# Second score pass of units over 512 keys in 64-row tiles of the TensorE array

## The chip, the cores and the metric

The kernel runs on one core of one Trainium2 chip. The metric is the device time of one execution in microseconds (us), the median of several runs; less is better.

## The reference, cut to what matters

One layer of a decoder trunk over 1024 positions of width 1024. The input is normalised and modulated (adaLN), projected to q, k and v of 8 stick-breaking heads and 8 forgetting heads (64 wide each), a gate path and 8 forget logits. The two kinds of attention give `o_sb` and `o_fx`, which are normalised, gated and projected back.

```python
def block(args):                       # stick-breaking, a block of 128 queries
    qb, i = args
    q_pos = i * Q_BLOCK + jnp.arange(Q_BLOCK)
    z = jnp.einsum('bhqd,bhkd->bhqk', qb, k).astype(jnp.float32) * scale
    causal = key_pos[None, :] < q_pos[:, None]
    log_rem = jnp.where(causal, jax.nn.log_sigmoid(-z), 0.0)
    after = lax.cumsum(log_rem, axis=3, reverse=True) - log_rem
    a = jnp.where(causal, jnp.exp(jax.nn.log_sigmoid(z) + after), 0.0)
    return jnp.einsum('bhqk,bhkd->bhqd', a.astype(v.dtype), v)
...
def block(args):                       # forgetting
    qb, cum_q, i = args
    q_pos = i * Q_BLOCK + jnp.arange(Q_BLOCK)
    logits = jnp.einsum('bhqd,bhkd->bhqk', qb, k).astype(jnp.float32) * scale
    logits = logits + cum_q[..., :, None] - cum[..., None, :]
    causal = key_pos[None, :] <= q_pos[:, None]
    p = jax.nn.softmax(jnp.where(causal, logits, -jnp.inf), axis=-1)
    return jnp.einsum('bhqk,bhkd->bhqd', p.astype(v.dtype), v)
```

## The kernel before

**Number format.** TensorE multiplies numbers of a rounded 32-bit format (fp32r, shown as f32 in the rows). To keep precision each operand is split into a rounded high part and a low rest, and a product is made of several passes that add up in one PSUM bank.

**Work.** The 16 heads form 8 pairs of two heads; even pairs are stick-breaking, odd pairs forgetting. A pair has 16 steps, one per unit g: head a of the pair, block qb (0 to 7) of 128 queries. `unit(g)` (L54) gives pair, head and block. A unit sees n = (qb + 1) * 128 keys, in pieces of up to 512 (`pieces`, L58): blocks 0 to 3 have one piece, blocks 4 to 7 have two, the second one of 128, 256, 384 or 512 keys. There are 128 units, 64 of them with two pieces.

**Scores.** The tile `stacks` (L180) holds for a buffer (p % 2) and a head three slots of 1024 columns over 128 partitions. Slot 0 is q, scaled, with its high part in partitions 0 to 63 and its low part in 64 to 127. Slot 1 is the high part of k in both halves of the partitions, slot 2 the low part of k in both. So the first pass of `scores` (L1314), q against slot 1, contracts over 128 rows and gives q_hi k_hi + q_lo k_hi, and the second pass (L1315), q against slot 2, gives q_hi k_lo + q_lo k_lo. The causal mask is added to the last 128 columns of a unit by a third, bf16, matmul (L1318). Each piece takes one of three PSUM banks in turn (`SCORE`, L224) and waits until the reader of the piece three before has freed it; `s_score` counts the finished pieces.

**Who reads them.** In `scores_out` of ScalarE (L757) a stick-breaking piece goes through two sigmoids (L767, L768); VectorE then scans (L1037) and GpSimd multiplies (L608). In `scores_out` of VectorE (L1033) a forgetting piece gets its forget term and row maximum (L1050), ScalarE takes the exponential (L772), VectorE the reciprocal (L1060), and GpSimd scales the row (L614). TensorE then transposes the probabilities (`transpose_probs`, L1342), ScalarE and VectorE copy them out as high and low part (L800, L1097), and TensorE multiplies them with the values (`values`, L1364).

**Order of the work.** Every engine has a program written out by hand as a loop over the units. On TensorE step g holds: half a projection unit of the next pair (`proj`, 12 matmuls of 512 columns at L1290, L1291, L1295), `scores(g + 2)`, on even steps `values` of the two units before, and `transpose_probs(g)`, which waits for GpSimd's `s_prob`. The last pair has output products (L1376) in place of most projections.

**Where q comes from.** `proj_out` of ScalarE (L717) copies the high part of a finished q projection from PSUM into slot 0 of both heads (L736, L737), then VectorE writes the low part (L1016) and so frees the bank. A q projection comes in two halves of 512 positions, `th` 0 and 1.

**Transfers by GpSimd.** From the end of pair 6 on, GpSimd issues 16 DMAs itself (`load_y_parts`, L573 to L579, and `load_wo`, L584 and L585), between its multiplications for the forgetting units.

Of the kernel before, what the change touches and what calls it, by code (L numbers as in the profile page):

```python
# [25 lines left out]
def hybrid_trunk_kernel(nc, x, c, w_ada_t, b_ada_cols, g_norm_cols, w_in, b_f_col, g_grp_cols, w_out, g_final,  # L26
                        identity, out):
    fp32 = mybir.dt.float32
    fp32r = mybir.dt.float32r
    bf16 = mybir.dt.bfloat16  # L30
    ALU = mybir.AluOpType
    ACT = mybir.ActivationFunctionType

    P = 128
    SEQ, D = x.shape
    HD = 64
    DC = D // P
    TB = SEQ // P
    HALF = 512
# [8 lines left out]
    SCALE = HD ** -0.5  # L48
    LOWEST = -3e38

    def is_sb(g):
        return (g // STEPS) % 2 == 0
# [5 lines left out]
    def pieces(g):  # L58

        n = (g % TB + 1) * P  # L60
        return [(a, min(a + HALF, n)) for a in range(0, n, HALF)]
# [49 lines left out]
    for g in all_units + [UNITS]:  # L111
        p, i = g // STEPS, g % STEPS
# [45 lines left out]
    with ctx:  # L158
        def sb(name, shape, dt=fp32):
            return ctx.enter_context(nc.sbuf_tensor(name, shape, dt))  # L160
# [17 lines left out]
        w_lo = sb("w_lo", [P, 2, DC, P], fp32r)  # L178

        stacks = sb("stacks", [P, 2, 2, 3, SEQ], fp32r)  # L180

        v_stack = sb("v_stack", [P, 2, 2, TB, P], fp32r)

# [14 lines left out]
        ident_bf = sb("ident_bf", [P, P], bf16)  # L198
        mask_f = sb("mask_f", [P, 2, P])
        mask_bf = sb("mask_bf", [P, 2, P], bf16)  # L200
# [59 lines left out]
        s_score = sem("s_score")  # L260
# [419 lines left out]
        def _(act):  # L680
# [36 lines left out]
            def proj_out(u, first=True, second=True):  # L717

                p, kind, th = units[u]
                bank = PROJ[proj_bank(u)]  # L720
                st = p % 2
                cols = slice(th * HALF, (th + 1) * HALF)
                if first:
                    act.wait_ge(s_proj, u + 1)
                if kind == "k":
                    for a in range(2):
                        src = bank[a * HD:(a + 1) * HD, :]
                        if a == 0 and first or a == 1 and second:
                            nc.scalar.activation(stacks[0:HD, st, a, 1, cols], src, ACT.Copy)
                            nc.scalar.activation(stacks[HD:P, st, a, 1, cols], src,  # L730
                                                 ACT.Copy).then_inc(s_phi if a else s_phk, 1)
                    return
                if not first:
                    return
                if kind == "q":
                    nc.scalar.activation(stacks[0:HD, st, 0, 0, cols], bank[0:HD, :], ACT.Copy, scale=SCALE)  # L736
                    nc.scalar.activation(stacks[0:HD, st, 1, 0, cols], bank[HD:P, :], ACT.Copy,  # L737
                                         scale=SCALE).then_inc(s_phi, 1)
                elif kind == "v":
                    if p == 0:  # L740
                        act.wait_ge(s_ada, 2 * DC)
                    if p >= 2:
                        act.wait_ge(s_tfree, T_ITEM["SS", p - 2, 0])
                    nc.scalar.activation(VT[:, cols], bank, ACT.Copy).then_inc(s_phi, 1)
                elif kind == "g":
                    if p == LAST:
                        act.wait_ge(s_wlo, len(blocks))
                    elif p >= 1:
                        act.wait_ge(s_yst, 16 * p)
                    else:  # L750
                        act.wait_ge(s_f, 4)
                    nc.scalar.activation(gate_of(p)[:, cols], bank, ACT.Sigmoid).then_inc(s_phi, 1)
                else:

                    nc.scalar.activation(CUM[1][0:8, cols], bank[F_LO:F_LO + 8, :], ACT.Copy).then_inc(s_phi, 1)
# [109 lines left out]
            for g in range(UNITS):  # L865
                p, i = g // STEPS, g % STEPS
# [389 lines left out]
        def _(pe):  # L1256
# [42 lines left out]
            def scores(g):  # L1299
                p, a, qb = unit(g)  # L1300
                q = stacks[:, p % 2, a, 0, qb * P:(qb + 1) * P]
                if g % STEPS == 0:
                    pe.wait_ge(s_plo, LO_UNITS[p, "k", 1])
                for j, (c0, c1) in enumerate(pieces(g)):
                    n = S_PIECE[g, j]
                    bank = SCORE[(n - 1) % 3]
                    if n > 3:
                        before = piece_list[n - 4]
                        if is_sb(before[0]):
                            pe.wait_ge(s_sig, SB_PIECE[before])  # L1310
                        else:
                            pe.wait_ge(s_logit, FX_PIECE[before])
                    diagonal = c1 == (qb + 1) * P
                    nc.tensor.matmul(bank[:, 0:c1 - c0], q, stacks[:, p % 2, a, 1, c0:c1], start=True, stop=False)  # L1314
                    last = nc.tensor.matmul(bank[:, 0:c1 - c0], q, stacks[:, p % 2, a, 2, c0:c1], start=False,  # L1315
                                            stop=not diagonal)
                    if diagonal:
                        last = nc.tensor.matmul(bank[:, c1 - c0 - P:c1 - c0], ident_bf[:],  # L1318
                                                mask_bf[:, 0 if is_sb(g) else 1, :], start=False, stop=True)
                    last.then_inc(s_score, 1)  # L1320

            def next_bank(item):
                n = T_ITEM[item]
# [178 lines left out]
```

## Time and profile before

| | us |
|---|---|
| median of 3 runs | 832.3 (832.14 to 835.11) |
| span of the profiled execution, first to last instruction | 828.7 |
| around that span in the profiled execution, taken from median less span | 3.6 |
| TensorE (PE) busy | 720.7 |
| weight loads (PEld) busy, beside PE | 604.4 |
| VectorE (DVE) busy | 490.9 |
| ScalarE (ACT) busy | 408.4 |
| GpSimd (POOL) busy | 390.7 |

The profiled execution's own time is not listed apart from its span; the last difference stands in for it. PE is TensorE's matmuls, PEld its loads of the stationary operand, DVE VectorE, ACT ScalarE, POOL GpSimd, SP the SyncE queue. A row of a timeline has the start, the duration, the engine, the line of the code, the operation with output and inputs, the shape, and in brackets the idle time of the engine just before with what ended it. Matmuls are pipelined, so one begins before the one ahead has ended: the pace is read from start to start, the duration has the way through the array in it.

### The profile page before, as it was taken

To read this page: it belongs to the slowest core of one execution; us is meant where nothing else is said; L and a number is where in the kernel's file an instruction comes from. 1 tells how busy PE (TensorE), PEld (TensorE's weight loads), DVE (VectorE), ACT (ScalarE), POOL (GpSimd) and SP (SyncE) were. 2 spreads that over 40 slices of the span, in tenths; PEclk is the share of its full clock that TensorE was granted. 3 is DMA by queue.
4 is the path that set the end of the run, shared out by engine and by line. 5 is a ranking of instruction groups with operands and counts; after the bars stand their busy time and mean duration, and the time that the engine had idled before them with its cause. 6 is when DMAs were issued, how large, how long until landed. Compare 5 with 4: busy or idle time off the path is not lost.

```text
span 828.7 us, 10998 instructions
## 1 busy us (share of the span) xinstructions
PE 720.7 (87%) x3936; PEld 604.4 (73%) x3936; DVE 490.9 (59%) x993; ACT 408.4 (49%) x846; POOL 390.7 (47%) x325
## 2 busy tenths in 40 slices
PE   0257965989999999999989989998899899999996
PEld 0146754768887887888777878887788788788884
DVE  1486663776564567756634676565447765545565
ACT  4027333576457555554645555555556465623132
POOL 2244422535866563467476644665556465221100
PEclk9988997999999999999989999999999999999998
DMA  6553332104245431133342411244432308894223
GB/s 185 183 200 148 129 100 40 35 22 86 98 102 138 108 103 26 26 91 102 88 136 57 102 26 26 77 128 127 152 94 67 85 25 304 243 311 166 68 90 128
DMA packets 64390, 91.57 MB, mean 111 GB/s; under 512 B 5448, under 2 KB 39880, under 8 KB 63824
## 3 DMA queue, kind: packets, MB, share of 16 engines
q1 hardware_dynamic: 57216, 72.17, 30.4%
q0 software_dynamic: 5376, 14.68, 5.6%
q10 hardware_dynamic: 1744, 4.02, 1.2%
q8 instruction: 32, 0.52, 0.2%
q14 instruction: 22, 0.18, 0.1%
HBM read 67.23 MB, written 23.63 MB: 110 GB/s over the span
## 4 chain that ended last, share of the span: by engine, by line
PE 34%; DMA 21%; POOL 19%; issue 9%; DVE 9%; ACT 6%; SPq 1%; DVEq 0%; POOLq 0%; ACTq 0%
DMA w_raw<-in_w_in 15%; PE psum L1376 10%; POOL w_lo L540 6%; DMA work<-in_w_ada_t 5%; PE psum L1290 4%; PE psum L1291 4%; PE psum L1295 4%; PE psum L1364 4%; DVE work L1037 3%; PE psum L1342 3%; POOL w_hi L534 3%; POOL work L554 2%; POOL work L608 2%; DVE stacks L1005 2%; POOL work L614 2%
## 5 line engine op out<-in xcount | busy, mean ns | idle before, releaser
L1290 PE MATMUL psum<-h_hi,w_hi 128*128 128x512 f32 x496 | 209.6, 423 | 23.9 <-POOL h_lo L591 13.5
L1295 PE MATMUL psum<-h_hi,w_lo 128*128 128x512 f32 x496 | 197.6, 398 | 0.0
L1291 PE MATMUL psum<-h_lo,w_hi 128*128 128x512 f32 x496 | 197.2, 398 | 0.0
L800 ACT ACTIVATE pt_hi<-psum 128x512 fp32r<-128x512 f32 (+1 forms) x192 | 87.5, 490 | 140.5 <-PE psum L1342 137.3
L1097 DVE TENSOR_TENSOR pt_lo<-psum,pt_hi 128x512 fp32r<-128x512 f32 (+1 forms) x192 | 100.6, 551 | 84.4 <-ACT pt_hi L800 83.4
L608 POOL TENSOR_TENSOR work<-work 128x127 f32<-128x127 f32 (+3 forms) x64 | 77.4, 1211 | 152.2 <-DVE work L1037 152.2
L1290 PEld LDWEIGHTS psum<-h_hi,w_hi 128*128 128x128 f32 x496 | 96.0, 193 | 43.6 <-issue 16.2
L1037 DVE TENSOR_TENSOR_SCAN work<-work 128x128 f32<-128x128 f32 (+3 forms) x64 | 104.1, 1627 | 32.5 <-ACT work L768 32.4
L1342 PE MATMUL psum<-ident,work 128*128 128x128 f32 x576 | 88.8, 282 | 29.9 <-POOL work L614 16.0
L1295 PEld LDWEIGHTS psum<-h_hi,w_lo 128*128 128x128 f32 x496 | 95.5, 192 | 22.2
L1291 PEld LDWEIGHTS psum<-h_lo,w_hi 128*128 128x128 f32 x496 | 96.1, 194 | 16.6
L1342 PEld LDWEIGHTS psum<-ident,work 128*128 128x128 f32 x576 | 63.5, 144 | 32.6 <-POOL work L614 17.3
L540 POOL TENSOR_TENSOR w_lo<-w_raw,w_hi 128x1024 fp32r<-128x1024 f32 x31 | 83.2, 2685 | 2.6
L772 ACT ACTIVATE work<-work,small 128x128 f32<-128x128 f32 (+3 forms) x64 | 49.8, 777 | 64.5 <-DVE small L1055 64.2
L1364 PE MATMUL psum<-pt_hi,v_stack 128*128 128x256 f32 x320 | 81.1, 288 | 0.4
L614 POOL TENSOR_SCALAR work<-work,small 128x128 f32<-128x128 f32 (+3 forms) x64 | 47.9, 749 | 68.6 <-DVE small L1060 68.5
L534 POOL TENSOR_SCALAR w_hi<-w_raw 128x1024 fp32r<-128x1024 f32 x31 | 34.5, 1112 | 94.6 <-DMA w_raw<-in_w_in 92.7
L1364 PE MATMUL psum<-pt_lo,v_stack 128*128 128x256 f32 x320 | 75.6, 283 | 0.0
L781 ACT ACTIVATE spare<-psum 64x256 f32<-64x256 f32 x64 | 24.4, 381 | 93.2 <-PE psum L1364 92.9
L1068 DVE TENSOR_TENSOR work<-psum,spare 64x256 f32<-64x256 f32 x64 | 26.7, 417 | 73.5 <-ACT spare L781 57.7
L1314 PE MATMUL psum<-stacks 128*128 128x512 f32 (+1 forms) x192 | 66.1, 345 | 4.4 <-ACT work L768 2.6
L1315 PE MATMUL psum<-stacks 128*128 128x512 f32 (+1 forms) x192 | 63.8, 345 | 0.0
(141 smaller groups left out, 1291.5 us busy)
## 6 DMA issues: line engine op xcount, KB each, us to landing
w_raw<-in_w_in SPq DMA_DIRECT2D x32, 512.0 KB, 9.4
work<-in_w_ada_t SPq DMA_DIRECT2D x24, 512.0 KB, 9.2
work<-in_x SPq DMA_DIRECT2D x16, 512.0 KB, 6.6
w_split_scratch<-work SPq DMA_DIRECT2D x16, 512.0 KB, 3.4
y_split_scratch<-work SPq DMA_DIRECT2D x10, 512.0 KB, 3.7
work<-forget_scratch SPq DMA_DIRECT2D x8, 512.0 KB, 5.1
work<-in_w_out SPq DMA_DIRECT2D x16, 256.0 KB, 5.6
stacks<-y_split_scratch POOLq DMA_DIRECT2D x4, 1024.0 KB, 6.7
```

Source lines behind the costliest of these rows:

```text
L540: nc.gpsimd.tensor_tensor(lo, w_raw[:], hi.bitcast(fp32), ALU.subtract).then_inc(s_wlo, 1)
L608: nc.gpsimd.tensor_tensor(U[g % 2][:, 0:n - 1], U[g % 2][:, 0:n - 1], R[g % 2][:, 1:n], ALU.mult).then_inc(s_prob, 1)
L800: nc.scalar.activation(pt_hi[:, a:e, (g % 2) * P:(g % 2 + 1) * P], bank, ACT.Copy).then_inc(s_thi, 1)
L1037: nc.vector.tensor_tensor_scan(R[g % 2][:, 0:n][:, ::-1], R[g % 2][:, 0:n][:, ::-1], R[g % 2][:, 0:n][:, ::-1], 1.0, ALU.mult, ALU.bypass) ...
L1097: nc.vector.tensor_tensor(pt_lo[:, a:e, q0:q0 + P], bank, pt_hi[:, a:e, q0:q0 + P].bitcast(fp32), ALU.subtract).then_inc(s_tfree, 1)
L1290: nc.tensor.matmul(bank, hi, h_hi[:, c_, cols], start=(c_ == 0), stop=False)
L1291: last = nc.tensor.matmul(bank, hi, h_lo[:, c_, cols], start=False, stop=(kind == "f" and c_ == DC - 1))
L1295: last = nc.tensor.matmul(bank, lo, h_hi[:, c_, cols], start=False, stop=(c_ == DC - 1))
L1314: nc.tensor.matmul(bank[:, 0:c1 - c0], q, stacks[:, p % 2, a, 1, c0:c1], start=True, stop=False)
L1342: last = nc.tensor.transpose(bank[:, (k - a) * P:(k - a + 1) * P], U[g % 2][:, k * P:(k + 1) * P], ident[:])
L1364: last = nc.tensor.matmul(OUT[:, c0:2 * P], v_stack[:, p % 2, a, k, :], src[:, k, c0:2 * P], start=(k == 0 and n == 0), stop=(k == qb + 1 ...
L1376: last = nc.tensor.matmul(psum[:, bank, :], y_, w_[:, m, cols], start=(j == 0 and k == 0), stop=(j == PAIRS // 2 - 1 and k == 2))
```

## The change

A new tile `q_again` holds the high part of the scaled q once more, in partitions 64 to 127, for both heads and for the positions 512 to 1023 (blocks 4 to 7). ScalarE writes it with two more copies of 64x512 whenever a q projection's half `th` = 1 is copied out.

A unit with two pieces is done in another order and with another second pass. Both pieces' first passes come first, into two banks. Then the second pass of the first piece contracts over partitions 0 to 63 only (q_hi against k_lo), and the second pass of the second piece over partitions 64 to 127 only (q_hi from `q_again` against the upper copy of k_lo). Then the mask. The small term q_lo k_lo is left out for these units. Units with one piece are as before. The number of matmuls is the same: five for a unit with two pieces.

The tile takes 8 KB of every partition (2 x 2 x 512 x 4 bytes). `dynamic_dma_scratch_size=4096` sets aside less of each partition for the descriptors of DMAs that GpSimd issues.

```diff
         stacks = sb("stacks", [P, 2, 2, 3, SEQ], fp32r)
+        q_again = sb("q_again", [P, 2, 2, HALF], fp32r)
...
                 if kind == "q":
                     nc.scalar.activation(stacks[0:HD, st, 0, 0, cols], bank[0:HD, :], ACT.Copy, scale=SCALE)
+                    if th == 1:
+                        for a in range(2):
+                            nc.scalar.activation(q_again[HD:P, st, a, :], bank[a * HD:(a + 1) * HD, :], ACT.Copy,
+                                                 scale=SCALE)
                     nc.scalar.activation(stacks[0:HD, st, 1, 0, cols], bank[HD:P, :], ACT.Copy,
                                          scale=SCALE).then_inc(s_phi, 1)
...
-                for j, (c0, c1) in enumerate(pieces(g)):
+                def whole(j, c0, c1):
                     n = S_PIECE[g, j]
                     bank = SCORE[(n - 1) % 3]
                     if n > 3:
...
-                    diagonal = c1 == (qb + 1) * P
                     nc.tensor.matmul(bank[:, 0:c1 - c0], q, stacks[:, p % 2, a, 1, c0:c1], start=True, stop=False)
-                    last = nc.tensor.matmul(bank[:, 0:c1 - c0], q, stacks[:, p % 2, a, 2, c0:c1], start=False,
-                                            stop=not diagonal)
-                    if diagonal:
-                        last = nc.tensor.matmul(bank[:, c1 - c0 - P:c1 - c0], ident_bf[:],
-                                                mask_bf[:, 0 if is_sb(g) else 1, :], start=False, stop=True)
-                    last.then_inc(s_score, 1)
+                    return bank
+
+                def mask(bank, c0, c1):
+                    return nc.tensor.matmul(bank[:, c1 - c0 - P:c1 - c0], ident_bf[:],
+                                            mask_bf[:, 0 if is_sb(g) else 1, :], start=False, stop=True)
+
+                if len(pieces(g)) == 1:
+                    (c0, c1), = pieces(g)
+                    bank = whole(0, c0, c1)
+                    nc.tensor.matmul(bank[:, 0:c1 - c0], q, stacks[:, p % 2, a, 2, c0:c1], start=False, stop=False)
+                    mask(bank, c0, c1).then_inc(s_score, 1)
+                    return
+                banks = [whole(j, c0, c1) for j, (c0, c1) in enumerate(pieces(g))]
+                first, second = pieces(g)
+                nc.tensor.matmul(banks[0], q[0:HD], stacks[0:HD, p % 2, a, 2, first[0]:first[1]], start=False,
+                                 stop=True).then_inc(s_score, 1)
+                nc.tensor.matmul(banks[1][:, 0:second[1] - second[0]],
+                                 q_again[HD:P, p % 2, a, qb * P - HALF:(qb + 1) * P - HALF],
+                                 stacks[HD:P, p % 2, a, 2, second[0]:second[1]], start=False, stop=False)
+                mask(banks[1], *second).then_inc(s_score, 1)
...
-    nc = bacc.Bacc("TRN2", target_bir_lowering=False, num_devices=1)
+    nc = bacc.Bacc("TRN2", target_bir_lowering=False, num_devices=1, dynamic_dma_scratch_size=4096)
```

How the change moves TensorE's program: unit 6 (pair 0, head 0, block 6, so pieces of 512 and 384 keys), before. L1295 is the end of a projection, L1364 the values of the units before. L1314 and L1315 are the two passes of a piece, L1318 the mask.

```order
L1295 MATMUL psum<-h_hi,w_lo 128x512
L1314 MATMUL psum<-stacks 128x512
L1315 MATMUL psum<-stacks 128x512
L1314 MATMUL psum<-stacks 128x384
L1315 MATMUL psum<-stacks 128x384
L1318 MATMUL psum<-mask_bf,ident_bf 128x128
L1364 MATMUL psum<-pt_hi,v_stack 128x256
```

The same place in the changed program. L1321 is the first pass, L1337 the second pass in the lower rows, L1339 that in the upper rows, L1326 the mask.

```order
L1302 MATMUL psum<-h_hi,w_lo 128x512
L1321 MATMUL psum<-stacks 128x512
L1321 MATMUL psum<-stacks 128x384
L1337 MATMUL psum<-stacks 128x512
L1339 MATMUL psum<-stacks,q_again 128x384
L1326 MATMUL psum<-mask_bf,ident_bf 128x128
L1386 MATMUL psum<-pt_hi,v_stack 128x256
```

The second piece's first pass has moved ahead of the first piece's second pass, and the two second passes stand side by side. Shapes name output partitions and columns, so the 64 rows do not show in them.

ScalarE's program where pair 1's q, half `th` = 1, is copied out, before (L736, L737). L767 and L768 are sigmoids, L781 the copy of values.

```order
L767 ACTIVATE work<-psum 128x256
L768 ACTIVATE work<-psum 128x256
L736 ACTIVATE stacks<-psum 64x512
L737 ACTIVATE stacks<-psum 64x512
L781 ACTIVATE spare<-psum 64x256
```

The same place in the changed program, with the copies at L739, L742 and L744.

```order
L774 ACTIVATE work<-psum 128x256
L775 ACTIVATE work<-psum 128x256
L739 ACTIVATE stacks<-psum 64x512
L742 ACTIVATE q_again<-psum 64x512 x2
L744 ACTIVATE stacks<-psum 64x512
L788 ACTIVATE spare<-psum 64x256
```

Two more copies stand between the two old ones, ahead of the signal that lets VectorE make the low part.

## Rows read from the trace of the kernel before

**Rows 1.** The page: the span in 40 slices, busy tenths (about 21 us each).

```profile
PE   0257965989999999999989989998899899999996
POOL 2244422535866563467476644665556465221100
PEclk9988997999999999999989999999999999999998
```

**Rows 2.** One stretch, 120 to 760 us, busy time of each engine.

```profile
120.00:760.00 640.00, 597.87 (x3375) 504.59 (x3376) 383.44 (x788) 346.30 (x738) 345.40 (x289) 0.98 0.37 103
```

**Rows 3.** Who TensorE waited for, 120 to 760 us: total, times, longest.

```profile
PE psum L1342 <- POOL work L614: 16.0, 9, 5.3
PE psum L1342 <- POOL work L608: 12.4, 4, 8.5
PE psum L1314 <- ACT work L768: 2.6, 2, 1.8
PE psum L1314 <- DVE small L1050: 1.8, 2, 1.6
```

**Rows 4.** Timeline of TensorE, a unit of 512 and 128 keys.

```profile
411.00 0.39 PE L1314 MATMUL psum<-stacks 128*128 128x512 f32 x1
411.23 0.39 PE L1315 MATMUL psum<-stacks 128*128 128x512 f32 x1
411.46 0.22 PE L1314 MATMUL psum<-stacks 128*128 128x128 f32 x1
411.51 0.28 PE L1315 MATMUL psum<-stacks 128*128 128x128 f32 x1
411.63 0.23 PE L1318 MATMUL psum<-mask_bf,ident_bf 128*128 128x128 bf16 x1
```

**Rows 5.** The same, units with second pieces of 256, 384 and 512 keys.

```profile
340.95 0.28 PE L1315 MATMUL psum<-stacks 128*128 128x256 f32 x1
341.07 0.23 PE L1318 MATMUL psum<-mask_bf,ident_bf 128*128 128x128 bf16 x1
...
344.96 0.34 PE L1315 MATMUL psum<-stacks 128*128 128x384 f32 x1
345.14 0.23 PE L1318 MATMUL psum<-mask_bf,ident_bf 128*128 128x128 bf16 x1
...
350.14 0.39 PE L1315 MATMUL psum<-stacks 128*128 128x512 f32 x1
350.37 0.23 PE L1318 MATMUL psum<-mask_bf,ident_bf 128*128 128x128 bf16 x1
```

**Rows 6.** Timeline of weight loads in the unit of rows 4.

```profile
411.23 0.19 PEld L1314 LDWEIGHTS psum<-stacks 128*128 128x128 f32 x1
411.46 0.19 PEld L1315 LDWEIGHTS psum<-stacks 128*128 128x128 f32 x1
```

**Rows 7.** Timeline of TensorE where a projection starts after a wait.

```profile
333.28 0.47 PE L1290 MATMUL psum<-h_hi,w_hi 128*128 128x512 f32 x1 [0.64 <-DVE stacks L1005]
333.58 0.40 PE L1291 MATMUL psum<-h_lo,w_hi 128*128 128x512 f32 x1
```

**Rows 8.** The copy of q by line (L737), and who ScalarE waited for, 120 to 760 us.

```profile
L737 ACT ACTIVATE stacks<-psum x16: 595/596/598, 75.8 to 625.6; 64x512 fp32r<-64x512 f32 x16
...
ACT pt_hi L800 <- PE psum L1342: 129.0, 63, 11.3
```

**Rows 9.** Timeline near 113 us, before the first scores are used.

```profile
111.27 3.38 DVE L954 CUSTOM_DVE_ANT_0 pt_lo<-work 128x1024 fp32r<-128x1024 f32 x1 [3.97 <-DMA work<-in_w_ada_t]
113.62 0.50 PE L1290 MATMUL psum<-h_hi,w_hi 128*128 128x512 f32 x1 [3.97 <-POOL w_lo L540]
```

**Rows 10.** A DMA that GpSimd issues (timeline), and its time to landing (DMA issues).

```profile
730.30 0.80 POOL L584 DMA_DIRECT2D h_lo<-w_split_scratch  x1
...
h_lo<-w_split_scratch POOLq DMA_DIRECT2D x4, 1024.0 KB, 7.7
```

## The prediction

> **What bounds the kernel now.** I read the page's slices first, then the busy time of the stretch in which the units run, then TensorE's waits in it, then its timeline inside single units. The slices show TensorE at 9 tenths or close to it from about 120 us on, at the full clock, while GpSimd moves between 4 and 8 [rows 1]. In the stretch from 120 to 760 us TensorE is busy 597.9 of 640 us, the next engine 383 us [rows 2]. So it stands still for 42.1 us in 640, and 28.4 us of that are 13 waits of the transposes for GpSimd's probabilities [rows 3]. Everything else there is TensorE at its own pace. A nanosecond taken from its stream in this stretch is a nanosecond off the end, unless it is taken just ahead of one of those few waits; a nanosecond added always shows. The change touches only the 64 units with two pieces, which all run in this stretch, 16 of each size.
>
> **Term 1, the second pass of the second piece goes under the first piece's.** The pace is start to start. Before, a pass of 512 keys takes 0.23 us (411.23 to 411.46) and the two passes of a unit's two pieces follow each other [rows 4]. The second pass of the second piece takes 0.12 us for 128 keys (411.51 to 411.63) [rows 4], and 0.12, 0.18 and 0.23 us for 256, 384 and 512 keys (341.07 less 340.95, and so on) [rows 5]. After, it stands in rows 64 to 127 of the array while the first piece's pass of 0.23 us is in rows 0 to 63. If the two run side by side it costs only what it hangs over. The second one cannot start before its weights are in. The nearest row for that lag is the one where a load and the matmul that uses it lie closest: the load of L1315 starts at 411.46 [rows 6] and its matmul at 411.51 [rows 4], 0.05 us. With that lag the passes of 128, 256 and 384 keys end within 0.23 us (0.05 + 0.18 = 0.23), and that of 512 hangs over by 0.05. Saved per unit: 0.12, 0.12, 0.18 and 0.18, together 0.60 us; times 16 is **9.6 us**. Bounds: nothing, if the two do not overlap, and 16 x 0.65 = 10.4 us without any lag.
>
> The Trainium skill, in "TensorE: Matmul & The Clock Gate", section "Measured speedup vs the span model", puts the lag between tiles of different rows at about 4 ns; by it this term would be about 10.3 us. No row of this trace shows matmuls in two row tiles.
>
> **Term 2, changing between 128 and 64 rows.** A changed unit goes from a 128-row first pass to 64-row tiles, and back for the mask: 2 changes x 64 units = 128 changes. The trace before has none, so I bound one. Below: nothing. A change of kind that the trace does have, from an f32 pass to the bf16 mask, costs nothing: 0.12 us after the pass of 128 keys, as the pace of such a pass is elsewhere, and 0.23 us after that of 512 [rows 4, 5]. Above: the array must be empty before it is set up anew. A matmul of 512 keys lasts 0.39 us from start to end and the next starts after 0.23 us [rows 4], so waiting for the end costs 0.16 us; then the weights, which now load under the running matmul [rows 6], come after it, another 0.05 us: 0.21 us. Between them lies the restart after a wait: the first matmul of a projection then takes 0.30 us to the next start, not 0.23 [rows 7], so 0.07 us are lost where weights were not loaded ahead. The three prices times 128 are 0, 9.0 and 26.9 us. I take **0**: the nearest row is the change of format within the same unit, where the next weights load under the running matmul all the same.
>
> **Term 3, the first piece is ready later.** `s_score` for the first piece now comes after the second piece's first pass, 0.05 to 0.23 us later, while the second piece is ready earlier. Its readers are two units ahead of the transposes, so mostly this is slack. It shows only where TensorE ends up waiting for the chain of that unit: 13 waits for GpSimd and a few shorter ones [rows 3]. At most 0.23 us at 15 places, 3.5 us, at least nothing. I take half, **+1.7 us**. The waits for a free score bank are 4.4 us in four places [rows 3], and the new order asks for the second bank only one pass earlier: within this term.
>
> **Term 4, ScalarE's copies.** 16 more copies of 64x512 at 0.596 us [rows 8] are 9.5 us on an engine that is busy 346 of 640 us [rows 2] and waited 129 us for the transposes [rows 8]. In a pair they come as 1.2 us at one step of sixteen, ahead of a bank that the next projection needs two units later. I cost them at nothing; without that cover each pair's step would slip 1.2 us, 8.3 us over seven pairs. The first two copies lie before the stretch, near 102 us, and hold up VectorE's low parts by 1.2 us. VectorE then waits 3.97 us for a load, and TensorE as long for GpSimd's weights, which depend on neither [rows 9]: absorbed.
>
> **Term 5, the smaller scratch.** GpSimd issues 16 DMAs of its own; one takes 0.80 us to issue and lands after 7.7 us [rows 10]. If the space still holds what is in flight, nothing changes, and I take nothing.
>
> **Sum.** 828.7 - 9.6 + 0 + 1.7 = 820.8 us of span, and with the 3.6 us around it **824.4 us**, 7.9 us under the median of 832.3, to which the profiled execution's span is tied by that same 3.6. A measurement of this kernel can tell about 0.5% from no change, 4.2 us.
>
> **Rival 1: the array is emptied at every change of tiling.** The mechanism is that of the upper bound: the 64-row load waits until the 128-row pass has gone through, and the mask's load until both tiles are done. Place: L1321 to L1337 and L1339 to L1326 in each of the 64 units, and nothing covers it, since TensorE is the bound [rows 2]. Price 26.9 us, time 824.4 + 26.9 = **851.3 us**. It breaks even at 7.9/128 = 0.06 us a change and is slower by over 0.5% from 0.095 us on; at 0.12 us it gives 839.8 us. For it: the long way through the array (0.16 us) [rows 4]. Against it: consecutive matmuls with other weights, formats and banks never wait for one another here [rows 4 to 6].
>
> The page "TensorEngine Tiling (Array Packing)" of the Trainium skill, section "Key Properties", says that a change of tiling mode, unlike one of tile, drains the TensorE. It gives no price; no row of this trace shows such a change. By that rule the time is that of this rival, and it is why I do not put it lower than I do.
>
> **Rival 2: only the prefetch of weights is lost at a change.** The array takes the new tiling on the fly, but a load for another tiling does not run under the matmul before. Price 9.0 us by the restart after a wait [rows 7], time **833.4 us**: within 0.5%. It would eat term 1 almost exactly.
>
> **Rival 3: the two 64-row passes run one after the other.** Then the change does not do what it says: as many columns stream as before, term 1 is nothing, and the time is 832.3 + 1.7 = **834.0 us**. For it: every matmul of this trace starts at the earliest when the one ahead has taken its columns. Against it: no two here are in different rows.
>
> **Rival 4: the smaller scratch makes GpSimd wait.** A second issue would wait for the first's landing, 7.7 - 0.8 = 6.9 us, in the four pairs of `load_wo`, ahead of the probabilities that TensorE's transposes need. With some 3 us of slack each this is 16 us: **840 us**. It needs descriptors for some MB in flight at a time, and loads are issued in twos.
>
> **Chances.** The forecast, 43%: it needs two things to go well, and both are what this trace shows of TensorE so far. Rival 1, 30%, anywhere from 0.095 to 0.21 us a change. Rival 2, 20%. Rival 3, 5%. Rival 4, 2%. The likeliest is the forecast, so 824.4. Its own range is 822 (no lag, half of term 3) to 827 (term 3 in full, 1 us of term 4). The whole range must reach into rival 1 to leave out no more than 2 in 10: from 821 to 847, where the top leaves out about the dearest third of it. Faster by over 0.5%: 43%. Within 0.5%: rivals 2 and 3, 25%. Slower by over 0.5%: rivals 1 and 4, 32%.
>
> **What would show it.** In the profile after: L1339 starting about 0.05 us after L1337 in every unit says term 1 is right; 0.23 us says rival 3. The time from L1321 of the second piece to L1337 beyond that pass's own pace (0.05 to 0.12, 0.12, 0.18, 0.23 us), and from L1339 to L1326 beyond what is left of the passes, is term 2: none says forecast, about 0.07 rival 2, 0.1 to 0.21 rival 1. TensorE's waits for GpSimd in 120 to 760 us should grow from 28.4 to about 30 us; if they grow by the whole of term 1, the gain went into the chain of the probabilities. The landing and issue times of L587 and L588 show rival 4. The forecast is wrong if a changed unit, from its first first pass to the matmul after the mask, is not 0.12 to 0.18 us shorter than before.

## The result and the profile after

The changed kernel is slower: 840.9 us median (839.24 to 842.08, 4 runs) against 833.7 us (4 runs), a ratio of 1.0098 with a 95% interval of 1.0078 to 1.0119. Two more comparisons, in other jobs, gave 1.0036 (1.0016 to 1.0057, 12 runs) and 1.0086 (1.0057 to 1.0116, 6 runs). It costs some 3 to 8 us; the forecast was 7.9 us faster. The profiled execution of the changed kernel took 840.04 us with a span of 838.2, so only 1.8 us lie around the span.

The page after, to be read beside [rows 1]:

```profile
span 838.2 us, 11014 instructions
PE 736.5 (88%) x3936; PEld 598.9 (71%) x3936; DVE 489.7 (58%) x993; ACT 417.4 (50%) x862; POOL 391.2 (47%) x325
PE   0257965989999999999989999998999899999996
PEclk9998988998999999999999999999999999899998
```

TensorE is busy 15.8 us longer although two passes of each changed unit now run side by side; ScalarE has its 16 copies more. TensorE's timeline in a unit of block 7 (512 and 512 keys), after. Two rows of the same line that overlap are shown as one with x2.

```profile
279.06 0.61 PE L1321 MATMUL psum<-stacks 128*128 128x512 f32 x2
279.61 0.50 PE L1337 MATMUL psum<-stacks 64*128 64x512 f32 x1
279.61 0.50 PE L1339 MATMUL psum<-stacks,q_again 64*128 64x512 f32 x1
280.04 0.23 PE L1326 MATMUL psum<-mask_bf,ident_bf 128*128 128x128 bf16 x1
```

The two 64-row passes do run side by side and start within 0.01 us of each other (279.61 both). But the two first passes, which take 2 x 0.23 us, are followed only after 0.55 us (0.09 more), and the pair of 0.23 us is followed by the mask only after 0.43 us (0.20 more). So the unit saves 0.23 us and pays 0.29. The weight loads in the same unit, to be read beside [rows 6]:

```profile
278.84 0.41 PEld L1321 LDWEIGHTS psum<-stacks 128*128 128x128 f32 x2
279.60 0.18 PEld L1337 LDWEIGHTS psum<-stacks 64*128 64x128 f32 x1 [0.35 <-issue]
279.61 0.18 PEld L1339 LDWEIGHTS psum<-stacks,q_again 64*128 64x128 f32 x1
280.04 0.10 PEld L1326 LDWEIGHTS psum<-mask_bf,ident_bf 128*128 128x128 bf16 x1 [0.24 <-issue]
```

Before, an f32 pass's load started with the matmul ahead of it [rows 4, 6]. Now the 64-row loads start 0.54 us after the first pass, with their own matmuls: they are not loaded ahead across the change. The 64-row pass lasts 0.50 us where one of 512 columns lasted 0.39 [rows 4]: 0.11 us of it is that load.

Over the 16 units of each block, the median from the start of the first pass to the start of the mask was 0.68, 0.69, 0.80 and 0.91 us before (blocks 4 to 7) and is 0.85, 0.865, 0.91 and 0.98 now. In block 4 every second unit stands behind the transposes of v, and its first pass takes 0.09 us longer in both kernels; like against like the unit is 0.18 us longer. So the units are 0.18, 0.17, 0.11 and 0.07 us longer, 0.53 together, times 16 is 8.5 us. The passes that no longer take time of their own are 0.12, 0.12, 0.18 and 0.23 us [rows 4, 5], 0.65 together. So the price is (0.53 + 0.65) / 4 = **0.30 us a unit, 0.15 us a change of tiling**: 18.9 us paid, 10.4 saved.

TensorE's waits from 120 to 760 us, after, beside [rows 3], and the busy time in that stretch, beside [rows 2]:

```profile
PE psum L1364 <- POOL work L611: 11.0, 3, 8.9
PE psum L1364 <- POOL work L617: 10.7, 6, 2.7
...
120.00:760.00 640.00, 605.69 (x3334) 492.71 (x3334) 378.43 (x775) 352.37 (x751) 343.21 (x286) 0.97 0.36 101
```

The waits for GpSimd fell from 28.4 to 21.7 us. A slower TensorE gave the others time, so part of the added stream was absorbed.

The same for pairs 1 to 6 alone, between the same instructions (the first transposes of v of pairs 1 and 7), before and then after:

```profile
197.99:676.79 478.80, 453.34 (x2592) 384.09 (x2593) 289.41 (x595) 264.04 (x570) 282.64 (x231) 0.99 0.32 87
```

```profile
205.08:685.54 480.46, 462.34 (x2593) 377.44 (x2593) 287.94 (x595) 270.72 (x582) 282.28 (x231) 0.98 0.32 87
```

TensorE is busy 9.0 us longer, of which the 48 changed units are 6.4, and stands still 7.3 us less, so the stretch is 1.7 us longer.

The spans differ by 9.5 us, more than the units' 8.5. Read at the transposes of v, which stand at fixed places of the program, the difference is made up so: 2.4 us by 127 us (1.2 of them in the input stage, before any changed instruction), 4.7 us in pair 0 (126.5 to 198.0 us, after 128.9 to 205.1), 1.7 us in pairs 1 to 6, 0.8 us behind. Pair 0 has only 8 of the changed units, 1 us. The rest there goes with the clock, seen in the stretch from 126 to 198 us, before and then after (the number behind the busy times is the granted clock):

```profile
126.00:198.00 72.00, 58.04 (x311) 47.66 (x309) 45.55 (x57) 41.48 (x86) 28.47 (x20) 0.93 0.22 45
```

```profile
126.00:198.00 72.00, 58.07 (x291) 45.93 (x290) 42.23 (x53) 39.49 (x81) 25.51 (x17) 0.88 0.23 45
```

0.05 less of full clock, between the levels of 2.4 and 1.2 GHz, is by estimate 7.2 us more at the lower level, worth 3.6 us. It follows an 8.9 us wait of TensorE near 140 us that the kernel before has too (8.5 us), and it comes and goes with the execution: profiles with 64-row tiles had 0.93 here, one without any had 0.88 (below).

### The profile page after: what moved, and what is told of

It is laid out like the page before. It is cut to its first block, busy times and chain, and to the rows that moved or that the text cites. A ratio compares the mean times of both kernels' runs of the same rounds, so it can differ in the third digit from the quotient of the medians.

```text
span 838.2 us, 11014 instructions
## 1 busy us (share of the span) xinstructions
PE 736.5 (88%) x3936; PEld 598.9 (71%) x3936; DVE 489.7 (58%) x993; ACT 417.4 (50%) x862; POOL 391.2 (47%) x325
## 4 chain that ended last, share of the span: by engine, by line
PE 43%; DMA 20%; POOL 15%; issue 8%; DVE 7%; ACT 6%; SPq 1%; DVEq 0%; POOLq 0%; ACTq 0%
DMA w_raw<-in_w_in 14%; PE psum L1398 11%; PE psum L1297 6%; PE psum L1302 6%; PE psum L1298 6%; POOL w_lo L543 5%; DMA work<-in_w_ada_t 5%; PE psum L1386 5%; PE psum L1364 4%; DVE work L1044 2%; PE psum L1321 2%; POOL w_hi L537 2%; DVE stacks L1012 2%; POOL work L617 2%; POOL work L557 2%
## 5 line engine op out<-in xcount | busy, mean ns | idle before, releaser
L1297 PE MATMUL psum<-h_hi,w_hi 128*128 128x512 f32 x496 | 212.5, 428 | 24.4 <-POOL h_lo L594 14.5
L1302 PE MATMUL psum<-h_hi,w_lo 128*128 128x512 f32 x496 | 201.6, 406 | 0.0
L1298 PE MATMUL psum<-h_lo,w_hi 128*128 128x512 f32 x496 | 200.5, 404 | 0.0
L1297 PEld LDWEIGHTS psum<-h_hi,w_hi 128*128 128x128 f32 x496 | 98.1, 198 | 44.9 <-issue 15.9
L1044 DVE TENSOR_TENSOR_SCAN work<-work 128x128 f32<-128x128 f32 (+3 forms) x64 | 102.4, 1601 | 32.2 <-ACT work L775 32.2
L1302 PEld LDWEIGHTS psum<-h_hi,w_lo 128*128 128x128 f32 x496 | 97.2, 196 | 22.7
L1298 PEld LDWEIGHTS psum<-h_lo,w_hi 128*128 128x128 f32 x496 | 97.9, 197 | 17.4
L1364 PE MATMUL psum<-ident,work 128*128 128x128 f32 x576 | 88.2, 281 | 22.6 <-POOL work L611 11.0
L1364 PEld LDWEIGHTS psum<-ident,work 128*128 128x128 f32 x576 | 63.2, 144 | 24.6 <-POOL work L611 12.2
L1386 PE MATMUL psum<-pt_lo,v_stack 128*128 128x256 f32 x320 | 75.5, 283 | 0.0
L1386 PEld LDWEIGHTS psum<-pt_hi,v_stack 128*128 128x128 f32 x320 | 61.9, 193 | 0.1
L1386 PEld LDWEIGHTS psum<-pt_lo,v_stack 128*128 128x128 f32 x320 | 61.5, 192 | 0.1
```

Source lines behind the costliest of these rows:

```text
L1044: nc.vector.tensor_tensor_scan(R[g % 2][:, 0:n][:, ::-1], R[g % 2][:, 0:n][:, ::-1], R[g % 2][:, 0:n][:, ::-1], 1.0, ALU.mult, ALU.bypass) ...
L1297: nc.tensor.matmul(bank, hi, h_hi[:, c_, cols], start=(c_ == 0), stop=False)
L1298: last = nc.tensor.matmul(bank, hi, h_lo[:, c_, cols], start=False, stop=(kind == "f" and c_ == DC - 1))
L1302: last = nc.tensor.matmul(bank, lo, h_hi[:, c_, cols], start=False, stop=(c_ == DC - 1))
L1364: last = nc.tensor.transpose(bank[:, (k - a) * P:(k - a + 1) * P], U[g % 2][:, k * P:(k + 1) * P], ident[:])
L1386: last = nc.tensor.matmul(OUT[:, c0:2 * P], v_stack[:, p % 2, a, k, :], src[:, k, c0:2 * P], start=(k == 0 and n == 0), stop=(k == qb + 1 ...
```

## The experiments

The first job asks whether the loss belongs to the change of tiling or to the pace of 64-row passes.

**Four pairs in a row.**

```diff
+                for k in range(4):
                     nc.tensor.matmul(banks[0], q[0:HD], stacks[0:HD, ...], start=False, stop=(k == 3))
                     nc.tensor.matmul(banks[1][...], q_again[HD:P, ...], stacks[HD:P, ...], start=False, stop=False)
                 mask(banks[1], *second).then_inc(s_score, 1)
```

> The pair of 64-row passes is issued four times in a row in each of the 64 units (three pairs too many, so the scores contain the term q_hi k_lo four times). In the changed kernel the pair starts together and the mask follows 0.43 us later, 0.20 us more than 512 columns take at 0.23. Theory A (a fixed price each time the array leaves the 64-row tiles): consecutive pairs start 0.23 us apart, and only the last one has 0.43 us before the mask; the time rises by 3 x 0.23 x 64 = 44 us to about 885. Theory B (64-row passes of this format stream at half pace, or two of them share one stream): every pair takes 0.43 us, the time rises by 3 x 0.43 x 64 = 83 us to about 923.

Measured: 881.6 us (one execution). TensorE's timeline in a unit of block 6:

```profile
321.50 0.56 PE L1321 MATMUL psum<-stacks 128*128 128x512 f32 x2
321.99 0.50 PE L1338 MATMUL psum<-stacks 64*128 64x512 f32 x1
...
322.33 0.39 PE L1338 MATMUL psum<-stacks 64*128 64x512 f32 x1
...
322.56 0.39 PE L1338 MATMUL psum<-stacks 64*128 64x512 f32 x1
322.62 0.34 PE L1342 MATMUL psum<-stacks,q_again 64*128 64x384 f32 x1
322.79 0.39 PE L1338 MATMUL psum<-stacks 64*128 64x512 f32 x1
323.12 0.23 PE L1326 MATMUL psum<-mask_bf,ident_bf 128*128 128x128 bf16 x1
```

Inside the tiling the pairs follow at 0.23 us, the full pace, with two streams at once. The first one has 0.34 us, 0.11 of it for weights that were not loaded ahead (it lasts 0.50, the next 0.39), and the last one 0.33, 0.10 of it waiting for the change back. The 1.13 us for four pairs are 0.43 + 3 x 0.23 to 0.01. The price is paid once per change, and theory B is out.

**Widths.** The lower pass takes 128 to 512 columns by block, the upper always 128; the rest of both second passes is left out.

```diff
-                nc.tensor.matmul(banks[0], q[0:HD], stacks[0:HD, p % 2, a, 2, first[0]:first[1]], ...)
+                nc.tensor.matmul(banks[0][:, 0:(qb - 3) * P], q[0:HD], stacks[0:HD, p % 2, a, 2, 0:(qb - 3) * P], ...)
```

> The lower pass takes 128, 256, 384 or 512 columns by block 4 to 7, the upper one always 128 (the rest of both second passes is left out). The gap from the lower pass to the mask: theory A, a fixed price: the columns at 0.45 ns each plus 0.20, so about 0.26, 0.31, 0.37 and 0.43 us. Theory B, half pace: 0.83 ns a column, about 0.11, 0.21, 0.32 and 0.43 us. The time: A about 841 - 16 x (0.17 + 0.12 + 0.06) = 835 us, B about 841 - 16 x (0.32 + 0.22 + 0.11) = 830 us.

Measured: 838.4 us (one execution). TensorE's timeline, lower pass and mask in blocks 4, 5 and 7:

```profile
298.71 0.32 PE L1337 MATMUL psum<-stacks 64*128 64x128 f32 x1
...
298.97 0.23 PE L1326 MATMUL psum<-mask_bf,ident_bf 128*128 128x128 bf16 x1
...
303.04 0.38 PE L1337 MATMUL psum<-stacks 64*128 64x256 f32 x1
...
303.35 0.23 PE L1326 MATMUL psum<-mask_bf,ident_bf 128*128 128x128 bf16 x1
...
312.57 0.50 PE L1337 MATMUL psum<-stacks 64*128 64x512 f32 x1
...
313.01 0.23 PE L1326 MATMUL psum<-mask_bf,ident_bf 128*128 128x128 bf16 x1
```

0.26, 0.31 and 0.44 us (0.36 in block 6): the columns at full pace and about 0.20 on top, as theory A has it. At half pace the first would be 0.11. The time is 3.4 us above theory A's 835 us, and 8.4 above theory B's; a single execution does not say where those 3.4 us went.

**One tile.** Only the first piece's second pass is in 64 rows; the other goes back to 128 rows.

```diff
-                nc.tensor.matmul(banks[1][...], q_again[HD:P, ...], stacks[HD:P, ...], start=False, stop=False)
+                nc.tensor.matmul(banks[1][...], q, stacks[:, p % 2, a, 2, second[0]:second[1]], start=False, stop=False)
```

> The first piece's second pass stays in the lower 64 rows, the second piece's goes back to 128 rows (with q_lo k_lo as before). So each unit still changes tiling twice but has nothing side by side. Theory A: 0.08 us lost on the way in and 0.20 on the way out, 0.43 us from the 64-row pass to the 128-row one; the time is 841 plus the second pieces' passes, 16 x (0.12 + 0.12 + 0.18 + 0.23) = 10.4 us: 851. Theory B by half pace of a 64-row pass: the same 0.43 us and time. Theory B by two passes sharing one stream: the single pass takes 0.23 us, the time is about 838.

Measured: 858.5 us (one execution), 7 more than theory A or the half pace gave and 20 more than a shared stream. TensorE's timeline, block 7:

```profile
319.80 0.50 PE L1337 MATMUL psum<-stacks 64*128 64x512 f32 x1
320.23 0.49 PE L1339 MATMUL psum<-stacks 128*128 128x512 f32 x1
320.56 0.23 PE L1326 MATMUL psum<-mask_bf,ident_bf 128*128 128x128 bf16 x1
```

A single tile pays the same 0.43 us, so running side by side has no part in the loss. And the f32 pass after the change back takes 0.33 us instead of 0.23: the load of its weights is open as well, which I had left out. 0.10 x 64 is 6.4 us, the 7 that were missing. Towards the mask nothing of this shows: its load starts with it in the kernel before as well, as the rows at term 2 below show, so there was no load ahead to lose.

**128 rows in the new order.** Order, copies and scratch as changed, both second passes over 128 rows.

```diff
-                nc.tensor.matmul(banks[0], q[0:HD], stacks[0:HD, p % 2, a, 2, first[0]:first[1]], ...)
+                nc.tensor.matmul(banks[0], q, stacks[:, p % 2, a, 2, first[0]:first[1]], ...)
...
-                                 q_again[HD:P, p % 2, a, qb * P - HALF:(qb + 1) * P - HALF], stacks[HD:P, ...], ...)
+                                 q, stacks[:, p % 2, a, 2, second[0]:second[1]], ...)
```

> The new order of the passes, ScalarE's copies into q_again and the smaller descriptor scratch are all kept, but both second passes contract over 128 rows as before: no 64-row tile. If the loss lies in the tiling (both theories), this is within 0.3% of the kernel before, 833 to 835 us, and the order costs under 2 us. A rival: the order, the copies or the scratch cost several us and the tiling is less to blame; then this is at 838 or more.

Measured: 835.1 us, ratio 1.0014 (0.9993 to 1.0036). All that the change does beside the tiles is worth no difference that these runs can tell. The interval reaches up to the 1.0036 that the changed kernel had in one of its comparisons, so the times alone do not put the loss on the tiles; the trace does: without them the units take 0.68, 0.69, 0.81 and 0.91 us from first pass to mask, as before to 0.01. This profile, without a tile, is the one with the clock of 0.88 in pair 0:

```profile
126.00:198.00 72.00, 58.57 (x298) 47.98 (x297) 43.03 (x54) 40.27 (x83) 25.54 (x17) 0.88 0.23 45
```

The second job varies the number and the neighbours of the changes.

**Block 7 only.** The other blocks are as in the kernel before.

```diff
+                last_block = qb == TB - 1
...
+                    if last_block:
+                        continue
                     last = nc.tensor.matmul(bank[:, 0:c1 - c0], q, stacks[:, p % 2, a, 2, c0:c1], ...)
...
+                if last_block:
+                    nc.tensor.matmul(banks[0], q[0:HD], stacks[0:HD, p % 2, a, 2, 0:HALF], ...)
+                    nc.tensor.matmul(banks[1], q_again[HD:P, p % 2, a, :], stacks[HD:P, p % 2, a, 2, HALF:2 * HALF], ...)
```

> 64-row tiles only for block 7, whose second piece has 512 keys and saves most (0.23 us by full overlap, against 0.12, 0.12 and 0.18 in blocks 4 to 6); the other units are as in the kernel before, and q_again holds 128 positions a head only. Theory A (each unit that changes tiling pays a fixed 0.28 to 0.29 us: about 0.19 in, 0.10 out to the bf16 mask): 16 x (0.28 - 0.23) = 0.8 us slower than before, so no difference that can be measured, ratio 0.999 to 1.003. A rival: the loss of the changed kernel comes from delays in the chain of the probabilities after the late first piece, which are worst in block 7; then at least a third of the 7 us stays, ratio 1.003 to 1.005.

Measured: 833.2 us, ratio 1.0020 (0.9997 to 1.0044): no difference that can be told, as theory A has it, though the interval does not shut the rival out. Even the block that gains most does not win.

**Mask first.**

```diff
+                mask(banks[1], *second, stop=False)
                 nc.tensor.matmul(banks[0], q[0:HD], ...).then_inc(s_score, 1)
                 nc.tensor.matmul(banks[1][...], q_again[HD:P, ...], ...).then_inc(s_score, 1)
-                mask(banks[1], *second).then_inc(s_score, 1)
```

> The mask goes ahead of the two 64-row passes instead of behind them, so that the array goes from the mask to the tiles, and from the tiles to an f32 matmul over 128 rows. Theory A, a change costs the wait for the array to run empty (0.10 us) plus the load of the next weights, which no longer lies under a running matmul (0.10 us for f32, little for bf16): on the way out 0.20 instead of 0.10 us, on the way in the mask's own uncovered load saves at most 0.06 us: 64 x 0.04 to 0.10 = 3 to 6 us more than the changed kernel, 844 to 847 us. Rival: a flat price per change whatever stands next to it: 841 us.

Measured: 835.6 us, ratio 1.0057 (1.0037 to 1.0077), faster than the 1.0098 of the changed kernel, and so a miss of both. Its timeline, block 4:

```profile
295.82 0.54 PE L1321 MATMUL psum<-stacks 128*128 128x512 f32 x2
296.20 0.23 PE L1326 MATMUL psum<-mask_bf,ident_bf 128*128 128x128 bf16 x1
296.36 0.50 PE L1338 MATMUL psum<-stacks 64*128 64x512 f32 x1
296.36 0.32 PE L1340 MATMUL psum<-stacks,q_again 64*128 64x128 f32 x1
296.79 0.38 PE L1387 MATMUL psum<-pt_hi,v_stack 128*128 128x256 f32 x1
297.01 0.28 PE L1387 MATMUL psum<-pt_lo,v_stack 128*128 128x256 f32 x1
```

The stream itself is as theory A had it: 0.97 us from the first pass to the values here, and the values' first pass takes 0.22 where it starts after a change; taken up to the second pass behind it, the median unit is 0.05 us longer than the changed kernel's, 3.3 us over the 64. That this did not show in the time is taken up below.

**Four changes.** Each 64-row pass stands behind its own first pass.

```diff
-                banks = [whole(j, c0, c1) for j, (c0, c1) in enumerate(pieces(g))]
+                banks = [whole(0, *first)]
                 nc.tensor.matmul(banks[0], q[0:HD], ...).then_inc(s_score, 1)
+                banks.append(whole(1, *second))
                 nc.tensor.matmul(banks[1][...], q_again[HD:P, ...], ...)
```

> Each changed unit goes 128 rows, lower tile, 128 rows, upper tile, mask: four changes instead of two and nothing side by side; the columns are those of the kernel with 128-row passes in the new order (835.1 us). Theory A, a price per change, additive: 0.19 in, 0.20 out to f32, 0.19 in, 0.10 out to the mask, 0.68 us x 64 = 43.5 us: about 878 us. Rival: the loss belongs to two tiles that run together (a shared stream or port), so that passes one by one cost their columns: about 835 to 840 us.

Measured: 867.7 us (one execution; the kernel before 830.9 in this job). Its timeline, block 7:

```profile
279.88 0.39 PE L1321 MATMUL psum<-stacks 128*128 128x512 f32 x1
280.20 0.50 PE L1337 MATMUL psum<-stacks 64*128 64x512 f32 x1
280.63 0.49 PE L1321 MATMUL psum<-stacks 128*128 128x512 f32 x1
281.05 0.49 PE L1340 MATMUL psum<-stacks,q_again 64*128 64x512 f32 x1
281.48 0.23 PE L1326 MATMUL psum<-mask_bf,ident_bf 128*128 128x128 bf16 x1
```

Four passes of 0.23 us take 0.32, 0.43, 0.42 and 0.43: 1.60 instead of 0.92, 0.68 us of changes, as expected to the hundredth. A 64-row pass alone pays like a pair. The time is 36.7 us above the kernel before in this job and some 10 us under the 878 expected. In pairs 1 to 6 the units are 32 us longer and the stretch 25 (504.0 against 478.8 us); the rest there went into idle time, 16.0 us instead of 25.5.

The third job asks why the mask ahead came out faster. All four ran on one chip, the kernel before at 832.1 us.

**The changed kernel again.**

> The changed kernel again, beside the others of this job, so that the differences of a few us between them rest on one chip. Both theories: ratio to the kernel before 1.008 to 1.011.

Measured: 835.4 us, ratio 1.0036 (1.0016 to 1.0057): below what I expected.

**The mask first, again.**

> The run with the mask ahead of the 64-row passes again. Its units are 0.06 to 0.08 us longer in TensorE's stream than the changed kernel's (3.7 us in all), yet it came out faster, 1.0057. Theory R (readiness): the second piece is signalled by its own 64-row pass and not by a mask that has to wait for the array, some 0.4 us earlier, so TensorE waits less for GpSimd's probabilities afterwards; then the ratio stays at or below 1.007, under the changed kernel's by 0.003 or more. Theory C (clock): the profiled and timed runs of the two differed in how much of pair 0 ran at the lower clock; then the two come out alike or this one slower, 1.009 to 1.014.

Measured: 836.2 us, ratio 1.0050 (1.0030 to 1.0071). Beside the changed kernel's 1.0036 it is the same or slower, so the order of the first two comparisons does not hold on one chip, and theory R's 0.003 is not there. Theory C has the order right, not the size.

**Block 7 only, mask first.** The three instructions of the block-7 run in the order of the run above.

> 64-row tiles for block 7 only and with the mask ahead of them. In TensorE's stream it costs 16 x 0.12 = 1.9 us. If an early second piece is worth something (theory R), then a quarter of the gain of the run before stays, some 2 us, and it is level with the kernel before, ratio 0.998 to 1.002. If not, 1.002 to 1.004.

Measured: 831.9 us, ratio 0.9999 (0.9979 to 1.0018). Level with the kernel before. That is the outcome that I had given to theory R, and the interval does not reach the 1.002 that I expected without it. But it does not tell this run from the other block-7 run (1.0020, 0.9997 to 1.0044) either, and the 0.12 us a unit are in its stream; they are 1.5 us for the 12 units in pairs 1 to 6, where the changed kernel's longer units are mostly absorbed as well. The next run tests theory R more directly.

**Late first piece.**

```diff
-                                 stop=True).then_inc(s_score, 1)
+                                 stop=True)
...
-                mask(banks[1], *second).then_inc(s_score, 1)
+                mask(banks[1], *second).then_inc(s_score, 2)
```

> The changed kernel with the first piece signalled together with the second one, at the mask, 0.4 us later than in the changed kernel; TensorE's stream is the same. Theory R: the readers of the scores are close enough to the transposes that this shows, TensorE's waits grow by up to 0.4 us at some 15 places, ratio at least 0.003 above the changed kernel's. If the readiness of the pieces is slack, the ratio is the changed kernel's within 0.002.

Measured: 834.5 us, ratio 1.0031 (1.0014 to 1.0049), against 1.0036 for the changed kernel beside it. Signalling the first piece 0.4 us later costs nothing that these runs can tell; theory R asked for at least 0.003 more, which the interval shuts out. When the first piece is ready is slack.

**The changed kernel a third time.**

> The changed kernel a third time, in a job of its own, because its first two comparisons with the kernel before disagree: 1.0098 (four executions) and 1.0036 (twelve). Theory S: TensorE's stream is 7.7 us longer and the waits for GpSimd take up part of that, so the true cost is 3 to 5 us, 1.003 to 1.006, and the first comparison had its few executions in the slow end of the scatter that pair 0's clock makes. Theory T: the whole 7.7 us shows and the second comparison was lucky: 1.008 to 1.010.

Measured: 839.3 us, ratio 1.0086 (1.0057 to 1.0116), six runs from 835.0 to 843.1. The medians alone settle neither theory. The stretches of the three profiles say more:

| | before | changed | second | third |
|---|---|---|---|---|
| pair 0, us (granted clock) | 71.5 (0.93) | 76.1 (0.89) | 75.5 (0.89) | 72.9 (0.93) |
| pairs 1 to 6, us | 478.8 | 480.5 | 479.7 | 480.1 |
| from there to the end, us | 151.9 | 152.7 | 152.9 | 152.8 |

In pairs 1 to 6 the units add 6.4 us and 0.9 to 1.7 show each time, so waits take up some 5 us. From there on the 8 units' 1.1 us show nearly in full (0.8 to 1.0), and pair 0 at the same clock is 1.4 us longer. Together that is 3 to 4 us, an estimate from one profile before and three after, and it speaks for theory S. What the clock in pair 0 and the stage before the units add is different from execution to execution; why two of the three comparisons came out at 7 to 8 us is not shown, since only one execution of each was profiled. That the change costs time is sure in all three comparisons, and where it is paid is seen in every unit. No version tried beats the kernel before.

## Why the prediction was wrong, point by point

- **What bounds the kernel.** TensorE, as said. But "a nanosecond added always shows" was too strong: the waits for GpSimd went from 28.4 to 21.7 us (the forecast had them grow to about 30), and pairs 1 to 6 lost 1.7 us where their 48 units have 6.4 us more. GpSimd's busy share, which I gave as 4 to 8 tenths, goes down to 2 or 3 in places [rows 1]; nothing hung on it.
- **Term 1** was right in kind and small by 0.8 us: no lag instead of 0.05 us, 10.4 us saved instead of 9.6. The upper weights load with the lower ones.
- **Term 2 is the step that failed.** It was taken as 0 between bounds of 0 and 0.21 us a change, "by the nearest row", the change of format from f32 to bf16. It measured 0.15 us, 18.9 us in all. I had also misread the row. I wrote that the mask's weights load under the running matmul; the same trace shows that they do not, in the unit of [rows 4]:

```profile
411.63 0.10 PEld L1318 LDWEIGHTS psum<-mask_bf,ident_bf 128*128 128x128 bf16 x1
```

```profile
411.67 0.36 PE L1364 MATMUL psum<-pt_hi,v_stack 128*128 128x256 f32 x1
411.87 0.28 PE L1364 MATMUL psum<-pt_lo,v_stack 128*128 128x256 f32 x1
```

The load starts with the mask (411.63 both), as it does at all 128 masks of that trace, where an f32 pass's load starts with the matmul ahead of it. Ahead of the mask that costs nothing to be seen, but the values' pass behind the mask takes 0.20 us where its like takes 0.12. Both kernels have this, so it does not enter their difference; it was a sign that loads are not always ahead. The two parts of my upper bound fit what was measured: a wait of 0.09 to 0.10 us (bounded at 0.16 by the modelled duration), which I read as the array running empty though no row shows its state, and the open load of 0.10 to 0.11 us (bounded at 0.05), which falls away towards the mask.
- **Rival 1** is what happened. At 0.148 us a change its own working gives 824.4 + 18.9 = 843.3 us; measured were 840.9, 835.4 and 839.3. The rule of the Trainium skill, "TensorEngine Tiling (Array Packing)", section "Key Properties", that a change of tiling mode drains the TensorE and a change of tile does not, agrees with these traces on both sides: 0.30 us a unit for the first, 0.23 us a pair with nothing on top for the second. I gave it 30% and the forecast 43%, on the strength of rows in which no change of tiling occurred.
- **Rival 2** had half of the mechanism, the open load, at 0.07 us. **Rival 3** is out: the passes start together. **Rival 4** is out: the loads by GpSimd take 0.80 us to issue as before and land after 7.5 us (7.7 before, [rows 10]).
- **Term 3**, +1.7 us, should have been nearer 0: with the first piece later by another 0.4 us the time was 834.5 us against 835.4, no longer.
- **Term 4** held in size: 16 copies at 0.593 us, and TensorE's wait behind the first of them grew from 1.45 to 2.65 us, just the 1.2 us said. Before, then after:

```profile
104.62 0.47 PE L1290 MATMUL psum<-h_hi,stacks 128*128 128x512 f32 x1 [1.45 <-DVE stacks L1016]
```

```profile
107.08 0.47 PE L1297 MATMUL psum<-h_hi,stacks 128*128 128x512 f32 x1 [2.65 <-DVE stacks L1023]
```

I had said that TensorE's next wait, for GpSimd's weights, would absorb it. In the second profile of the changed kernel it did (2.32 us instead of 3.97); in this one it was 4.51 us, because the weights themselves came later, so this profile does not show it. With order and scratch together they stay under what 1.0014 (0.9993 to 1.0036) can tell.
- **The base.** I tied the profiled span to the median by 3.6 us; around a span lie 1.8 us, so that execution was a fast one of its kernel. The forecast as a difference from the median does not change by it.
- **Range and chances.** 840.9 us lies in the range of 821 to 847, which was there for this rival; the sign was wrong. A changed unit came out 0.07 to 0.18 us longer up to the mask, where the forecast had it 0.12 to 0.18 us shorter.

## What to carry to other kernels

Work in 64-row tiles pays only if one visit to that tiling saves more than it costs to get there and back, here 0.30 us, or some 650 columns at the pace of 512 in 0.23 us: gather several passes into a visit, and go back through the bf16 mask rather than an f32 matmul (0.10 against 0.20 us in TensorE's stream; the two orders' times, 835.4 and 836.2 us, could not be told apart). Where the trace before has no instance of a change of mode, a row that is near it in the program is no evidence for "free", and that row's own loads have to be looked at; price it by what the engine does ahead of time in normal running (here the load of weights) and ask whether that can go on across the change. Before a difference of a few us is explained by a mechanism, repeat both kernels side by side: here an order seen between two separate jobs did not hold on one chip.

## What the runs showed that I had not expected

Two f32 passes in different 64-row halves run at full pace together, starting within 0.01 us of each other, also four pairs in a row (0.23 us each). An f32 pass that follows a change of tiling is longer than usual by the load of its own weights (0.49 to 0.50 us of duration instead of 0.39), in either direction, while the bf16 mask is not: its load is never ahead, at no mask of the kernel before either. And the first pair's 72 us varied by about 4.7 us between profiles, 1 us of it the units; the rest goes with the granted clock there, from 0.88 to 0.93, with tiles (76.1 us against 72.9) and without (74.4 us at 0.89 in the run with 128 rows, 71.5 at 0.93 before).
